# Hymba block with PEER experts on one core: 96 tokens gathered in two kinds of row tiles, 160 dense

## What is computed

```
q = (hc @ wq).reshape(T, PEER_HEADS, 2, PEER_KEY_DIM)
s1 = einsum('thd,hnd->thn', q[:, :, 0], sub_keys[:, 0])      # 128 keys each
s2 = einsum('thd,hnd->thn', q[:, :, 1], sub_keys[:, 1])
v1, i1 = top_k(s1, 16);  v2, i2 = top_k(s2, 16)
cand = v1[..., :, None] + v2[..., None, :]                   # 16 x 16
sc, ci = top_k(cand, 16)
e = take(i1, ci // 16) * 128 + take(i2, ci % 16)             # expert numbers
g = softmax(sc)
act = gelu(einsum('td,thkd->thk', hc, exp_u[e]))
out = einsum('thk,thkd->td', g * act, exp_v[e])
```

## Time and profile before

| | |
|---|---|
| median of 3 runs | 847.19 us (846.68 to 847.84) |
| the profiled execution's own time | 847.16 us |
| its span | 845.4 us |
| PE busy | 819.9 us (97%) |
| DVE busy | 560.8 us (66%) |
| ACT, POOL busy | 171.8 us (20%), 208.6 us (25%) |
| moved by DMA | 286.39 MB, mean 339 GB/s |
| granted TensorE clock, mean | 0.994 |

### The profile page before, as it was taken

The page is one execution under the profiler, slowest core; times in us unless marked ns, Lnnn a source line. Parts: engine busy times, 40 slices in busy tenths (PEclk is TensorE's granted clock), DMA queues, the critical chain, the costliest instruction groups (busy, mean ns, idle before and its releaser), DMA issues.

```text
span 845.4 us, 14556 instructions
## 1 busy us (share of the span) xinstructions
PE 819.9 (97%) x5758; PEld 783.5 (93%) x5758; DVE 560.8 (66%) x1134; ACT 171.8 (20%) x449; POOL 208.6 (25%) x216
## 2 busy tenths in 40 slices
PE   6999999999989999999999999999999999999996
PEld 4998879888979999999999999989999999999996
DVE  4959889698994998688788898554553344343302
ACT  4454575542111112121111111000000000000003
POOL 2000000000104321655434436533222323322100
PEclk9999999999999999999999999999999999999998
DMA  9998781653898998999999999999999999999951
GB/s 336 405 373 333 328 371 78 274 187 114 226 273 276 411 409 290 382 408 409 409 393 365 361 393 377 410 408 409 409 409 409 378 408 391 389 388 398 342 174 50
DMA packets 75909, 286.39 MB, mean 339 GB/s; under 512 B 9483, under 2 KB 11707, under 8 KB 74562
## 3 DMA queue, kind: packets, MB, share of 16 engines
q1 hardware_dynamic: 48482, 191.00, 59.1%
q0 software_dynamic: 27360, 94.47, 29.6%
HBM read 283.90 MB, written 1.52 MB: 338 GB/s over the span
## 4 chain that ended last, share of the span: by engine, by line
PE 86%; DMA 7%; DVE 5%; ACT 1%; issue 1%; ACTq 0%; SPq 0%; DVEq 0%
PE banks L1223 35%; PE banks L1194 32%; DMA raw<-in_u_t 3%; PE banks L941 3%; PE banks L1206 2%; PE banks L859 2%; PE banks L894 2%; PE banks L937 2%; DMA raw<-in_w_mod 2%; DMA raw<-in_v_b 2%; PE banks L1010 1%; PE banks L864 1%; DVE sc_w L1330 1%; PE banks L910 1%; PE banks L1242 1%
## 5 line engine op out<-in xcount | busy, mean ns | idle before, releaser
L1223 PE MATMUL banks<-act,raw 128*128 128x168 f32 x2048 | 306.1, 310 | 0.4
L1223 PEld LDWEIGHTS banks<-act,raw 128*128 128x128 f32 x2048 | 294.8, 191 | 10.4 <-DMA raw<-in_v_b 10.4
L1194 PE MATMUL banks<-hT,raw 128*128 128x168 f32 x2048 | 298.4, 307 | 3.2 <-DMA raw<-in_u_t 3.1
L1194 PEld LDWEIGHTS banks<-hT,raw 128*128 128x128 f32 x2048 | 292.3, 190 | 4.7 <-DMA raw<-in_u_t 4.7
L1696 DVE SCALAR_TENSOR_TENSOR row_sums<-rows,weight,row_sums 128x1024 f32<-128x1024 f32 x85 | 109.2, 1285 | 142.7 <-DMA rows<-in_v_b,idx 124.0
L541 POOL DMA_INDIRECT rows<-in_u_rows,idx x88 | 109.4, 1243 | 128.1 <-DVE dots L1673 91.7
L541 POOL DMA_INDIRECT rows<-in_v_b,idx x88 | 86.2, 980 | 179.7 <-PE banks L1223 142.5
L1673 DVE CUSTOM_DVE_ANT_0 rows<-rows,h_rows 128x1024 f32<-128x1024 f32 x88 | 105.9, 1221 | 18.7 <-issue 13.4
L791 ACT ACTIVATE turned<-banks,ccol 128x256 f32<-128x256 f32 x8 | 3.8, 473 | 293.6 <-PE banks L1223 293.6
L749 ACT ACTIVATE act<-banks 128x168 f32<-128x168 f32 (+20 forms) x121 | 33.1, 273 | 121.5 <-PE banks L1194 114.8
L508 POOL DMA_DIRECT2D h_lines<-h_stage x1 | 0.5, 541 | 211.4 <-ACT h_stage L774 211.4
(11 more groups left out here) (238 smaller groups left out, 825.5 us busy)
## 6 DMA issues: line engine op xcount, KB each, us to landing
raw<-in_u_t SPq DMA_DIRECT2D x128, 512.0 KB
raw<-in_v_b SPq DMA_DIRECT2D x128, 512.0 KB
wq<-in_wq SPq DMA_DIRECT2D x2, 4096.0 KB, 18.2
sh_w<-in_w_mod SPq DMA_DIRECT2D x8, 512.0 KB, 13.2
sc_w<-in_w_mod SPq DMA_DIRECT2D x8, 512.0 KB, 13.4
win<-in_w_in SPq DMA_DIRECT2D x8, 512.0 KB, 14.1
win<-in_w_in SPq DMA_DIRECT2D x1, 4096.0 KB, 20.8
sc_w<-in_w_mod SPq DMA_DIRECT2D x2, 2048.0 KB, 23.4
```

The lines of the kernel that those rows point to most:

```text
L1194: last = nc.tensor.matmul(dst, raw[n % RAW][:, c * P:(c + 1) * P], hT[:, c, 0:MANY], start=(c == 0), stop=(c == DC - 1))
L1223: return nc.tensor.matmul(chunk_place(c)[:, 0:MANY], raw[(BLOCKS + j) % RAW][:, c * P:(c + 1) * P], act[:, j, :], start=(j == 0 and c < 4) ...
```

## The change

- `KINDS` becomes (64, 32): 96 tokens are gathered in two kinds, 160 are dense. So there are 96 tiles of U and 96 of V, the matmuls of U and V move 160 columns, and there are 20 groups of gates.
- The two loads of `h2_rows` go from POOL's queue to SP's, behind the stream's loads 15 and 16 (`H2_LOAD`), and the h2 transposes from U block 4 to 2 (`H2_AT`).
- `part` holds each digit twice, side by side, and the compare of L1742 runs over pairs.
- The last product with the keys goes behind U block 0; the banks of the query products rotate the other way (`query_banks`), and block 0 waits for the query product before the last (`q_sum` 5).
- `EARLY` 18 to 24, with two dot products at each place in the sort; `TURN_AT`, `GATE_AT` and `EXP_AT` some blocks later; `PACE` 1.45 to 1.36.

Core of the diff (constants and unchanged lines cut):

```diff
-KINDS = (64, 16, 8)
+KINDS = (64, 32)
...
-EARLY = 18
+EARLY = 24
...
-H2_AT = 4
-EXP_AT = 50
+H2_AT = 2
+H2_LOAD = 15
+EXP_AT = 54
...
-TURN_AT = 55
-GATE_AT = 60
+TURN_AT = 60
+GATE_AT = 65
...
-PACE = 1.45
+PACE = 1.36
...
         part_u = at("part_u", 13312 + 1024, [P, 2, HEADS, TOPK], U32)
-        part = at("part", 13312 + 1280, [P, 2, HEADS, TOPK], F16)
+        part = at("part", 13312 + 1280, [P, 2, HK, 2], F16)
         chosen = at("chosen", 13312 + 1536, [P, TT, 3, HK])
...
         raw_full = [sem(f"raw_full{n}") for n in range(RAW)]
+        h2_in = loaded["sh2a"]
         table_built, table_out, out_done = map(sem, ("table_built", "table_out", "out_done"))
...
             sem, ("second_ready", "onehot_ready", "gates_ready", "gates_used", "gates_out"))
-        lines_moved = sem("lines_moved")
+        lines_moved, h2_saved = map(sem, ("lines_moved", "h2_saved"))
         gathered = [sem(f"gathered{n}") for n in range(SLOTS)]
...
 
-        H2_SAVED, H2_IN, EXPERTS_SAVED, IDX_IN, FEW_SAVED, FEW_IN = 16, 64, 80, 128, 144, 192
+        EXPERTS_SAVED, IDX_IN, FEW_SAVED, FEW_IN = 16, 48, 64, 96
 
...
 
-            return (6, 2, 4)[(g - 2) % 3]
+            return (6, 4, 2)[(g - 2) % 3]
 
...
                              ).then_inc(raw_full[n % RAW], 16)
+                if 0 <= n - H2_LOAD < len(KINDS):
+                    kind, count = n - H2_LOAD, KINDS[n - H2_LOAD]
+                    sp.wait_ge(h2_saved, 16)
+                    sp.dma_start(h2_rows[kind][:, :],
+                                 bass.AP(tensor=h2_lines, offset=KIND_AT[kind] * D,
+                                         ap=[[0, P // count], [D, count], [1, D]])).then_inc(h2_in, 16)
             sp.dma_start(final_gb[:, :], final_g.broadcast_to([P, D])).then_inc(fin_in, 16)
...
             pool.wait_ge(xn_ready, TT + 3)
-            pool.dma_start(h2_lines.ap(), h2_stage[0:FEW, :]).then_inc(lines_moved, 16)
-            pool.wait_ge(lines_moved, H2_SAVED)
-            for n, count in enumerate(KINDS):
-                pool.dma_start(h2_rows[n][:, :],
-                               bass.AP(tensor=h2_lines, offset=KIND_AT[n] * D, ap=[[0, P // count], [D, count], [1, D]])
-                               ).then_inc(lines_moved, 16)
-
+            pool.dma_start(h2_lines.ap(), h2_stage[0:FEW, :]).then_inc(h2_saved, 16)
             def spread_lines(dst, lines):
...
             for g in range(2, LISTS // 2):
-                if g == 4:
+                if g == 3:
                     pe.wait_ge(proj_out, N_IN + 2)
...
                 query_wide(WQ + g, g)
-                if g in QUAD_AFTER:
+                if g in QUAD_AFTER[:-1]:
                     key_scores(QUAD_AFTER.index(g))
...
                     pe.wait_ge(act_out, n - 1)
+                if n == 0:
+                    pe.wait_ge(q_sum, LISTS // 2 - 3)
                 dst = bank[4 + n % 2][:, 0:MANY]
...
                 if n == H2_AT:
+                    pe.wait_ge(s_out, TT * LISTS // 4)
                     for c in range(DC):
...
                 u_block(n)
+                if n == 0:
+                    key_scores(len(QUAD_AFTER) - 1)
             for j in range(BLOCKS - LAST):
...
                 if i == 0:
-                    ve.wait_ge(lines_moved, H2_IN)
+                    ve.wait_ge(h2_in, 16 + 16 * len(KINDS))
                 tile = row_tile(i)
...
                 if places[0] > SORT_SKIP and dotted[0] < EARLY:
-                    some_dots(min(2 - places[0] % 2, EARLY - dotted[0]))
+                    some_dots(min(2, EARLY - dotted[0]))
 
...
                                              ALU.bitwise_and))
-                link(nc.vector.tensor_copy(part[:, :, :, :], part_u[:, :, :, :]))
+                link(nc.vector.tensor_copy(part[:, :, :, :], spread(part_u[:, :, :, :].rearrange("p n h k -> p n (h k)"), 3, 2)))
                 for half in range(2):
 
-                    place = spread(spread(place_h[:, :], 1, TOPK), 1, HEADS)
-                    link(nc.vector.tensor_tensor(hit[:, :, :, :], spread(part[:, half], 3, TOPK), place,
-                                                 ALU.is_equal))
+                    place = spread(place_h[:, :].rearrange("p (q two) -> p q two", two=2), 1, HK)
+                    link(nc.vector.tensor_tensor(hit[:, :, :, :].rearrange("p h k (q two) -> p (h k) q two", two=2),
+                                                 spread(part[:, half], 2, TOPK // 2), place, ALU.is_equal))
                     between()
```

## The result

The changed kernel takes 849.19 us (median of 14, 846.11 to 851.13) against 846.69 us for the kernel before in the same measurement (14 runs, 840.85 to 848.72). The ratio is 1.0036, 95% interval 1.002 to 1.0051: slower, by more than the 0.2% that can be told. The forecast was 836.1 us and faster.

A forecast was written before the change was run, and what follows sets the result against it. DMA at 409 GB/s was taken as the bound while gathers lag, with PE's limit within a few per cent. U part -13.6, V part +4.9 and end -2.4 sum to -11.1 us, hence 836.1 us; range 828 to 847.

The forecast's parts named there:

- term 4: h2 row loads beside the U blocks: 4.2 us lost as before, a change of 0, bounds -4.2 to +11.
- The rule that stood against the change: h2 loads, leading repeat limiting engines: 15.4 us in the stream's queue less 8 of buffer, a stall of 7, 839 us.
- The upper bound of 15: h2 loads in the stream's queue: two loads of up to 11.4 us each, a stall of 15 us, +11.
- Terms 1 and 2: U blocks: narrower matmuls, 2.176 us a block, -13.7 us over 128 blocks; one gate group fewer, -0.9 us.
- term 6: Gate groups in the U blocks: DVE keeps up on average, late groups hold PE by tenths, +0.5 us (0 to 3).
- Term 3: Start of the U blocks: block 0 fills PE's 1.48 us wait ahead of the last scores, -1.5 us.
- term 5: Early gathers beside the U blocks: stream slowed to 2.44 us a block for about 25 blocks, +2 us (0 to +5).
- The U part: U blocks up to the V blocks: the six terms together -13.6 us, V blocks beginning at 510.5.
- The V part: V blocks up to `few_sums`: DMA decides, 231.3 tiles in 296.5 us plus 2 idle, 298.5 us, +4.9.
- The end: `few_sums` with 32 instructions of 48, -2.0 us, and the last four blocks, -0.4: -2.4 in the sum.
- the two rivals with a stall of more than 4.2 us: h2 loads: stall 2 to 6 us over the 4.2, 838 to 842 us, 0.20; or 15 us, 847 us, 0.11.
- full stall: Rival: the stream stalls the full 15 us at the h2 loads, 847 us; chance 0.11.

The follow-up runs named there:

- the kernel with copies: Against the changed kernel, h2 rows loaded copy by copy (2 + 4 loads without a repeat) at the same place in SP's queue: 834.5 us, ratio 0.986.

## Why the prediction was wrong

The step that failed is term 4, "Less to load and a worse place: I keep 4.2 us, a change of 0". In its place stands a stall of 11.7 us at blocks 16 and 17, and it falls away whole when the repeat is taken out of the load (834.5 and 835.05 us). The rule that stood against the change had the mechanism: the Trainium skill ("DMA: Bandwidth & Descriptors", Rules for kernel authors) says that a leading repeat of c copies confines a load to at most c engines. The traces agree: 0.29 of DMA busy at 72 GB/s about PE's second wait, from 232 to 239 us 196 GB/s for 334 once the repeat was gone, and two and four landings for the two loads where loads without a repeat have 16. I had made the rule a rival and kept 4.2 us, against it the high share of 0.90 at 268 GB/s. That row mixed three loads with a stream that had a queue to itself and filled the other engines. In one queue the other engines went on too, at 0.86 and 241 GB/s from 239 to 246 us, but every block has a share behind the h2 rows on the few engines that carry them. The prediction's working by the rule, 15.4 us in the queue and a stall of 7, was still short: from the first issue to the last landing the two loads took 25.1 us (226.36 to 251.47). It left out the stream's own shares on those engines; whether that is all of the difference is open. The upper bound of 15 held.

Term by term, in the traced executions:

- **Terms 1 and 2**: right. A block takes 2.174 us (2.176 forecast); 68 blocks, 20 groups and six transposes between the turn and the V blocks would be 147.8 + 18.4 + 0.7 = 166.9 us and took 168.3 (353.94 to 522.23). So 1.4 us are lost there where the kernel before lost 0.8, and term 6, late groups, is +0.6 for +0.5.
- **Term 3**: right, and cheap: no wait at the scores. The transposes behind block 1 did not wait. Block 1 starts at 205.36, 0.8 us sooner than counted, but that is spread between executions: with the same order it starts at 206.22 in the kernel with copies.
- **Term 4**: 11.7 us for 4.2, and behind it the 1.7 of clock that stand in term 5's stretch.
- **Term 5**: mis-sized, 7.5 us for 2 and the 0.4 that the kernel before lost there. 1.7 of it is PE's clock, at half from 253.95 to 257.37 us after the second wait; the other 5.8 are what the kernel with copies loses in the same stretch, 6.0. I had counted 25 blocks at 2.44 us, less 4 us of cover. In the chain the stream's tiles set the pace from 280.94 to 323.37 us, some 16 blocks at 2.56, and each is lost in full: the cover was used up before they began. Also "gates ready at 331 to 338" came out at 345.00: DVE was done at 330.4, but the exponentials stand behind the gelu of block 54, which came late. PE didn't wait for it, as its block 60 came at 354; DMA's gap of 261 GB/s, which I said would fill, filled by half: 327 GB/s from 314 to 346 us.
- **The U part**: -1.7 us (522.40 for 524.14 at its end) for -13.6, 11.9 too much. Terms 4 to 6 came to 11.7 + 7.5 + 1.4 = 20.6 us lost where the kernel before loses 5.4 (4.6 from block 4 to its turn at 336.51, 0.8 behind it): +15.2 for the +2.5 forecast, 12.7 too much, less the 0.8 of term 3.
- **The V part**: right. 299.9 us (522.40 to 822.26) for 298.5, at 409 GB/s while gathers lag. "Here the change gives back what the narrower V matmuls would save" is what happened.
- **The end**: -5.6 us for -2.4. `few_sums` fell by 2.6, and the rest is PE's clock, below.

Sum: -1.7 + 6.2 - 5.6 = -1.1 us, the change of the span. Without the stall the kernel is at 834.5, within 2 us of the 836.1 forecast, though by errors that cancel, which is luck: against the forecast, term 4 is at -4.2, term 5 at +3.6, the V part at +2.4 and the end at -3.1.

The chances were off in one place: the two rivals with a stall of more than 4.2 us held 0.31, and neither was joined to a heavier term 5. The "full stall" at 847 us is the nearest to what came.

## What to carry to other kernels

Before a load moves into the queue of a stream that must not stop, look at how many engines it can use: here a repeat of 2 or 4 as the outermost dimension put it on two or four, and every block behind it in the queue was late by its shares on those. Split such a load into copies, or repeat on the write; in the kernel before, copies in SP's queue gave 0.5%, in the changed one 1.8%. A low rate at a high DMA share is no proof that a single load uses all engines: ask what else was running, and set the cover of the buffers (five blocks, 10.9 us) against the whole time from the loads' first issue to their last landing (25.1 us here).

## What the hardware showed that I had not expected

**TensorE's clock at the end.** Three kinds need 48 narrow matmuls in `few_sums`, two need 32. Windows of the kernel before, then of the change, around them and the 16 instructions behind:

```profile
818.00:824.00 6.00, 6.00 (x47) 6.00 (x47) 0.00 (x0) 0.00 (x0) 0.00 (x0) 0.83 0.02 6
824.00:829.00 5.00, 5.00 (x20) 4.95 (x20) 0.00 (x0) 0.89 (x2) 0.00 (x0) 0.52 0.00 0
```

```profile
822.20:825.80 3.60, 3.60 (x34) 3.60 (x33) 0.00 (x0) 0.00 (x0) 0.00 (x0) 1.00 0.06 25
825.80:828.00 2.20, 2.20 (x18) 2.20 (x18) 0.00 (x0) 0.47 (x1) 0.00 (x0) 1.00 0.03 7
```

Before, the granted clock fell to 0.52, near the lower of its two levels, 1.2 GHz, and the 16 instructions took 4.68 us; now it stays at 1.00, 2.4 GHz, and they take 2.26. With 88 tokens in the kernel with copies they take 4.06 again. So dropping a kind came with 2.4 us, 0.1 of them from the narrower matmuls, that no term counted.

**The clock after a standstill.** The stall cost more than its waits. After 6.74 us without work block 16 took 4.63 us for 2.34, and the granted clock from 246 to 252 us is 0.62. After the second wait it fell again (windows as above):

```profile
252.00:254.00 2.00, 1.11 (x8) 1.11 (x9) 2.00 (x17) 0.00 (x0) 1.34 (x2) 0.99 0.63 254
254.00:256.00 2.00, 2.00 (x9) 2.00 (x9) 1.97 (x15) 0.00 (x0) 0.17 (x1) 0.50 0.40 66
256.00:258.00 2.00, 2.00 (x11) 2.00 (x11) 2.00 (x17) 0.30 (x1) 0.00 (x0) 0.66 0.29 78
258.00:260.00 2.00, 2.00 (x17) 2.00 (x16) 1.24 (x9) 0.30 (x1) 0.44 (x1) 1.00 0.70 256
```

From 253.95 to 257.37 us the clock is at 0.50, though PE had begun block 17 at 252.89: 9 and 11 instructions in 2 us where 17 are usual, 1.7 us lost. In the kernel with copies nothing of the kind happens in the U blocks.

**Two queues that are both behind share evenly.** With gathers and stream both waiting, PE takes 2.56 us a block, which is two tiles of 1.282 us: one of each. From 274 to 316 us DMA moves 409 GB/s, PE does 277 instructions, 17 blocks, and POOL issues 16 gathers. What an early gather costs U depends on the slack left: six more (18 to 24) cost 2.7 of their 7.7 us of DMA, the next four 3.3 of 5.1.
